# Latent attention of a two-block network: the mask as rows of the score product, and values one unit later

## The reference, cut to what matters

```python
def chunk_ids(L):
    p = jnp.arange(L)
    return jnp.where(p < N_META, 0, 1 + (p - N_META) // CHUNK)      # N_META 16, CHUNK 64
...
    def one_block(args):
        qblk, qc = args
        s = jnp.einsum('bqhd,bkhd->bhqk', qblk, k).astype(jnp.float32) * scale
        mask = cid[None, :] <= qc[:, None]
        p = jax.nn.softmax(jnp.where(mask, s, -jnp.inf), axis=-1).astype(v.dtype)
        return jnp.einsum('bhqk,bkhd->bqhd', p, v)
```

## Time and profile before

| | us |
|---|---|
| median of 3 runs | 2048.93 (2047.54 to 2051.88) |
| the profiled execution's own time | 2042.87 |
| its span, from first to last instruction | 2040.9 |
| PE busy | 1943.8 (95%), 11408 instructions |
| PE's weight loader busy | 1692.7 (83%) |
| DVE busy | 1049.4 (51%) |
| ACT busy | 753.8 (37%) |
| mean granted clock of TensorE | 0.973 |

### The profile page before, as it was taken

One profiled execution on the slowest core, in us unless ns is written; L12 is line 12 of the kernel. 1 busy time (PEld: TensorE's weight loads), 2 busy tenths in 40 slices (PEclk: granted clock), 3 DMA queues, 4 the chain that ended last, 5 costly groups with the idle time before them and its releaser, 6 DMA issues.

```text
span 2040.9 us, 28553 instructions
## 1 busy us (share of the span) xinstructions
PE 1943.8 (95%) x11408; PEld 1692.7 (83%) x11408; DVE 1049.4 (51%) x1480; ACT 753.8 (37%) x1232; POOL 33.0 (2%) x31
## 2 busy tenths in 40 slices
PE   8999998999999997999999999999787999999997
PEld 8887788999999996888888777777686898888886
DVE  5644374664444458544444666676426253323335
ACT  5354342432232434423223425553445352212222
POOL 0100000100000000000000000000000000000000
PEclk9999999999999998999999999999778999999998
DMA  5211101233222332232223232222001223223221
GB/s 180 65 61 42 55 1 52 83 94 93 92 84 92 93 94 93 83 104 93 92 93 94 79 106 73 73 73 83 1 1 63 93 73 103 94 84 102 94 84 61
DMA packets 46607, 161.87 MB, mean 79 GB/s; under 512 B 4832, under 2 KB 7136, under 8 KB 46368
## 3 DMA queue, kind: packets, MB, share of 16 engines
q1 hardware_dynamic: 46208, 158.60, 24.5%
q10 hardware_dynamic: 288, 1.70, 0.2%
HBM read 156.09 MB, written 4.19 MB: 79 GB/s over the span
## 4 chain that ended last, share of the span: by engine, by line
PE 88%; DVE 6%; ACT 3%; DVEq 1%; issue 1%; DMA 0%; ACTq 0%; SPq 0%
PE ps L446 76%; PE ps L944 2%; PE ps L860 1%; DVE wlo L2126 1%; PE ps L964 1%; PE ps L833 1%; DVE W L2519 1%; PE ps L575 1%; PE ps L831 1%; PE ps L1107 1%; DVE AM L2305 1%; PE ps L1070 0%; PE ps L1104 0%; ACT RR L1960 0%; PE ps L1097 0%
## 5 line engine op out<-in xcount | busy, mean ns | idle before, releaser
L446 PE MATMUL ps<-UH,whi 128*128 128x264 f32 (+2 forms) x1920 | 655.1, 341 | 10.7 <-DVE wlo L2126 9.2
L446 PE MATMUL ps<-UL,whi 128*128 128x264 f32 (+2 forms) x1920 | 646.8, 337 | 0.0
L446 PE MATMUL ps<-UH,wlo 128*128 128x264 f32 (+3 forms) x1632 | 530.8, 325 | 0.0
L1351 ACT ACTIVATE whi<-raw 128x1024 fp32r<-128x1024 f32 x284 | 297.8, 1053 | 444.6 <-PE ps L446 424.8
L446 PEld LDWEIGHTS ps<-UH,whi 128*128 128x128 f32 x1920 | 365.0, 190 | 53.2 <-issue 12.6
L446 PEld LDWEIGHTS ps<-UL,whi 128*128 128x128 f32 x1920 | 364.7, 190 | 40.2 <-issue 2.4
L446 PEld LDWEIGHTS ps<-UH,wlo 128*128 128x128 f32 (+1 forms) x1632 | 309.6, 190 | 25.2
L2126 DVE TENSOR_TENSOR wlo<-raw,whi 128x1024 fp32r<-128x1024 f32 x248 | 308.1, 1245 | 39.7 <-ACT whi L1351 39.5
L446 PE MATMUL ps<-HH,whi 128*128 128x264 f32 (+1 forms) x768 | 246.4, 321 | 0.0
L446 PE MATMUL ps<-HL,whi 128*128 128x264 f32 (+1 forms) x768 | 246.3, 321 | 0.0
L446 PE MATMUL ps<-HH,wlo 128*128 128x264 f32 (+1 forms) x768 | 245.7, 320 | 0.0
(11 more groups left out here) (437 smaller groups left out, 2356.3 us busy)
## 6 DMA issues: line engine op xcount, KB each, us to landing
raw<-W SPq DMA_DIRECT2D x284, 512.0 KB, 3.5
H<-xT SPq DMA_DIRECT2D x4, 528.0 KB, 6.5
spill<-H SPq DMA_DIRECT2D x1, 2048.0 KB, 8.9
H<-spill SPq DMA_DIRECT2D x1, 2048.0 KB, 8.6
MEM<-memT ACTq DMA_DIRECT2D x1, 1024.0 KB, 4.7
out<-H SPq DMA_DIRECT2D x2, 512.0 KB, 2.9
out<-H SPq DMA_DIRECT2D x4, 256.0 KB, 3.1
masks<-masks SPq DMA_DIRECT2D x1, 768.0 KB, 9.9
```

The source lines that it names most:

```text
L446: mm = pe.matmul(dst, a, b, start=start and n == 0, stop=stop_ and n == 2)
L1351: act.activation(whi[s % NB][:, :, :], raw[s % NB][:, :, :], ACT.Copy).then_inc(w_hi, 1)
```

## The change

- The queries' rotary rows `QR` and the keys' rotated rows `KRS` become rows 0 to 63 of two tiles of 68 rows, `QRX` and `KRX`. Rows 64 to 67 stand for the four groups of 128 frames. In `QRX` row 64 + g is 1 for the first 64 tokens of group g, in `KRX` it is -1e30 for the last 64 tokens of group g, and both are 0 elsewhere. The product of the two adds -1e30 just where the mask wants it.
- The 20 mask products (16 units, in four of them two) are gone, and `early` with them.
- The four rows come with the rotary table from HBM by two DMAs that ACT issues, one for each tile, each to 4 partitions by 4 heads by 528 tokens. The first score waits for them.
- On PE a unit's place now holds `values(x - 1)`, `score(x + 1)`, `turned(x)`, and `values(19)` comes after the last. On ACT `output(x - 1)` stands ahead of `copies(x)`, and `output(19)` at the end.

```diff
-        early = masks[0:1, LEVELS + 3:LEVELS + 5, :].rearrange("p a t -> p (a t)")[:, 64:64 + P]
...
+        QR, KRS = QRX[0:ROPE, :, :], KRX[0:ROPE, :, :]
...
                 if x:
                     pe.wait_ge(M["exp"], x)
+                else:
+                    pe.wait_ge(rope_in, 48)
...
-                    mm = pe.matmul(flat[0:n, 2048 + a:2048 + b], QR[:, h, q0:q0 + n], KRS[:, h, a:b], start=False,
+                    mm = pe.matmul(flat[0:n, 2048 + a:2048 + b], QRX[:, h, q0:q0 + n], KRX[:, h, a:b], start=False,
                                    stop=True, skip_group_check=True)
-
-                    c = max(a, nk - 64)
-                    if j and c < b:
-                        mm = pe.matmul(flat[0:n, 2048 + c:2048 + b], early, ones[0:1, 0:b - c], start=False, stop=True,
-                                       skip_group_check=True)
...
             def unit(x):
-                turned(x)
+                if x:
+                    values(x - 1)
                 if x + 1 < HEADS * NCH:
                     score(x + 1)
-                values(x)
+                turned(x)
...
                 unit(2 * y + 1)
+            values(HEADS * NCH - 1)
...
             head_rstd(0)
             head_rstd(1)
+            for x, to in enumerate((QRX, KRX)):
+                act.dma_start(to[ROPE:ROPE + 4, :, :], rope_d[ROPE:ROPE + 4, x:x + 1, :].to_broadcast([4, HEADS, L])
+                              ).then_inc(rope_in, 16)
             weights_hi(FT["z3"])
...
             for x in range(HEADS * NCH):
+                if x:
+                    output(x - 1)
                 copies(x)
                 if x + 1 < HEADS * NCH:
                     exps(x + 1)
-                output(x)
...
+            output(HEADS * NCH - 1)
...
+    t, block = np.arange(L)[None, :], META + P * np.arange(4)[:, None]
+    early = np.where((t >= block) & (t < block + 64), 1.0, 0.0)
+    late = np.where((t >= block + 64) & (t < block + P), BIG, 0.0)
+    return np.ascontiguousarray(np.stack([np.concatenate([c, c, early]), np.concatenate([s, s, late])], 1).astype(np.float32))
```

More of the change, by code:

```diff
@@ L183, in build @@
         turn = masks[0:ROPE, LEVELS + 3, 0:ROPE]
-        early = masks[0:1, LEVELS + 3:LEVELS + 5, :].rearrange("p a t -> p (a t)")[:, 64:64 + P]
         future = masks[:, LEVELS + 4, :]
-        ZH, KN, QR, KRS, VT, KR, TAB, SR0, SR1, KSQ, SN, stat = region(
-            S0, ("ZH", [P, 16, L], F32), ("KN", [P, HEADS, L], F32), ("QR", [ROPE, HEADS, L], F32),
-            ("KRS", [ROPE, HEADS, L], F32), ("VT", [P, 5, 512], F32), ("KR", [ROPE, L], F32),
+        ZH, KN, QRX, KRX, VT, KR, TAB, SR0, SR1, KSQ, SN, stat = region(
+            S0, ("ZH", [P, 16, L], F32), ("KN", [P, HEADS, L], F32), ("QRX", [ROPE + 4, HEADS, L], F32),
+            ("KRX", [ROPE + 4, HEADS, L], F32), ("VT", [P, 5, 512], F32), ("KR", [ROPE, L], F32),
             ("TAB", [ROPE, 2, L], F32), ("SR0", [ROPE, L], F32), ("SR1", [ROPE, L], F32), ("KSQ", [ROPE, L], F32),
             ("SN", [ROPE, L], F32), ("stat", [P, 16], F32))
+        QR, KRS = QRX[0:ROPE, :, :], KRX[0:ROPE, :, :]
         hw = S0 + 16 * L * 4
@@ L350, in _ @@
                     sp.dma_start(masks[:, :, :], masks_d[:, 0:LEVELS + 5, :]).then_inc(consts_in, 16)
-            sp.dma_start(TAB[:, :, :], rope_d).then_inc(rope_in, 16)
+            sp.dma_start(TAB[:, :, :], rope_d[0:ROPE, :, :]).then_inc(rope_in, 16)
             sp.dma_start(ABW[:, :, :], gates_d).then_inc(N["ab_in"], 16)
@@ L2995, in constants @@
     turn = np.where(t == s - half, -1.0, 0.0) * (s < ROPE) + np.where(t == s + half, 1.0, 0.0) * (t < ROPE)
-    early = np.where((s == 0) & (t >= 64), BIG, 0.0)
-    masks += [s == t, s <= t, s >= 0, turn + early, np.where(s > t, BIG, 0.0)]
+    masks += [s == t, s <= t, s >= 0, turn, np.where(s > t, BIG, 0.0)]
     for l in range(1, LEVELS + 1):
@@ L3010, in rope_table @@
     c, s = np.cos(ang), np.sin(ang)
-    return np.ascontiguousarray(np.stack([np.concatenate([c, c]), np.concatenate([s, s])], 1).astype(np.float32))
+    t, block = np.arange(L)[None, :], META + P * np.arange(4)[:, None]
+    early = np.where((t >= block) & (t < block + 64), 1.0, 0.0)
+    late = np.where((t >= block + 64) & (t < block + P), BIG, 0.0)
+    return np.ascontiguousarray(np.stack([np.concatenate([c, c, early]), np.concatenate([s, s, late])], 1).astype(np.float32))
 def pack(i):
```

## The result

| | before | after |
|---|---|---|
| median of the timed runs | 2048.23 us (4 runs, 2047.35 to 2051.88) | 2031.66 us (4 runs, 2030.52 to 2035.68) |
| ratio | | 0.9919, 95% interval 0.9901 to 0.9938 |
| profiled execution | 2042.87 us, span 2040.9, clock 0.973 | 2035.68 us, span 2033.4, clock 0.972 |
| first score to the first product of the HGRN scan | 124.80 us | 114.88 us |

The profile shows most of the steps that it named, and two that it did not: shorter groups of transposes, and a fall of the clock just behind the stage.

A forecast was written before the change was run, and what follows sets the result against it. TensorE (PE) was taken as the bound, ending the chain for 88% of the span. PE's work -7.2, waits +0.7 and clock -1.1 gave -7.6 us, applied to the median 2048.93: 2041.3 us, range 2037.0 to 2047.0.

The forecast's parts named there:

- mask products and steps in the score groups: Attention score groups: dropping 20 mask products and using 68 rope rows saves 2.69 us a head, 10.8 us in four.
- 16-row values product: First values product of a unit now follows a 128-row z product, a 0.2 us step in 18 groups: +3.6 us.
- units 9 and 14: Last units of heads 1 and 2: values' waits of 0.55 us go, transposes wait 0.3 more; 0.2 gained each, -0.4.
- unit 19: Last unit: with no score in between, its transposes wait for ACT's output copy, +0.6 us.
- unit 6: Output copy 5 stands behind ACT's scaling and DVE's maximum comes later, so PE waits: +0.5 us.
- unit 4, apart from the clock and the terms above: End of head 0: transposes wait for ACT's output copy behind Silu, but the chain starts sooner; counted as even.
- clock: Attention stage: two paid falls go (-3.0), a likely one at unit 4 (+0.8); half of -2.2 taken, -1.1 us.
- The 0.20 that was to come back: 144-column score group: the step out of the 16-row transposes falls on the z tile behind, returning 0.20 us.
- The first rival: Rope product's load is not pulled ahead, so only the mask products go: -2.4 us, 2046.5 us; chance 0.12.
- The second: Two more clock falls than now are paid, with transposes between short products and z tile: 2045.4 us; chance 0.13.
- The third: ACT's output copy stands behind its side work and delays PE: +11.4 us, 2060.3 us; chance 0.05.
- Waits in sum: PE's waits in the attention stage: heads 1 and 2 -0.4, last unit +0.6, unit 6 +0.5, together +0.7 us.

The follow-up runs named there:

- after_w8: The changed kernel with an already met wait for the rope tables written 9 times instead of once before the first scores; 2037.68 us, 0.9960 of before.
- rows_only: The changed kernel with its mask rows but the order of values and scores from before; 2033.92 us, 0.9946 of before.

## Why the prediction was wrong in size, point by point

The result's own medians lie 16.6 us apart. All runs of the two kernels together give 2044.97 (72 runs) to 2032.31 us (nine), -12.7 us, and by span times clock 1986.7 to 1977.1, -9.6. The lower clock took 56.9 us of a run before and 54.2 after, by the means, another 2.7.

| step | predicted | measured |
|---|---|---|
| mask products and steps in the score groups | -10.8 | -11.2, by differences of starts (-11.0 without the 16-key group) |
| 16-row values product | +3.6 | +3.8, longer values groups and entries |
| transposes ahead of a z tile | not counted | -1.6 |
| units 9 and 14 | -0.4 | -0.8 (0.55 gone, 0.17 new, each) |
| unit 19 | +0.6 | +0.4 |
| unit 6 | +0.5 | 0: no wait at that unit |
| unit 4, apart from the clock and the terms above | 0 | -0.1 (its head takes 32.12 less 2.7 against 31.82, and 2.3 of that are the products) |
| new transfers | 0 | 0 |
| sum without the clock | -6.5 | -9.5 by the rows, -9.6 by the runs |
| clock | -1.1 | -2.7 by the means of all runs, against a scatter of some 10 us of single runs; +2.4 between the two profiled executions |
| sum | -7.6 | -12.2 (-12.7 between the medians) |

The stage's own ends agree: 124.80 less the 3.1 us of its falls, and 114.88 less 2.7, lie 9.5 us apart.

**Right** were the terms that carry the argument: the size of each score group, the step of 0.2 us, that 68 rows behave like 128, and the places of the waits. The load runs 0.42 us ahead of its product, not some 0.1. The 0.20 that was to come back on the z tile behind the 16-row transposes is 0.02 (0.23 against 0.21). The first rival (the rotary product stays a bare one) falls with the load at 139.37. The second (the clock keeps falling) is only half refuted. There is one fall in the stage and not three, and the mean of all runs went the way of the forecast. But both kept executions of the changed kernel pay a second fall behind the stage, which the prediction did not look for when it let nothing downstream move. They have 0.972 as their clock, and six of the nine have 0.973 to 0.975, so not every run need pay it; after_w8, which differs in eight idle waits, has none there. The rival's cause, though, is not what is seen. The short values, transposes and 0.17 us of wait at unit 9 had no fall behind them. By the rule of the Trainium skill's page TensorE: Matmul & The Clock Gate, Part 4 (PE-mode transpose), that transposes do not keep the clock up, as the prediction read it, it would have fallen there. The trace does not bear that reading out for a group of five transposes. The third (ACT's queue on the path) falls with the table of waits: the transposes wait in four units, not in most.

**The steps that failed are three.** First, the sum lacks a term. The prediction costed what each moved group pays on the way in, and not what the group behind it gets. It took the transposes at the length that they had ahead of a score, and they are 1.6 us shorter ahead of a z tile. Second, "Waits in sum: -0.4 + 0.6 + 0.5 = +0.7" was -0.5: unit 6 was a guess between three durations close to one another, and it came out on the free side, while units 9 and 14 gained twice what was taken. These two are 2.8 us of the miss. Third, "I apply the sum to the median" put the forecast on 2048.93 us, the median of three runs, although the profiled execution lay 6.1 us below it. 72 runs have 2044.97, so this base was 4.0 us high, and only 1.5 of uncertainty had been allowed for it. With the 1.6 by which the clock took less than forecast, these make 8.4 of the 9.6 us between forecast and result. That share of the clock is luck in part: in the two profiled executions it went the other way. The rest is inside the scatter of four runs.

That all of the 3.6 us belong to the move was a reason only partly right, with the right number (3.8). The 16-row product pays wherever 68 rows or more stand ahead of it, and without the mask products they do in both orders: in rows_only 0.09 in each of four score groups and 0.17 in the values of a head, 2.1 us in four heads.

## What to carry to other kernels

Count PE's products by what stands next to them, not one by one: here a change from 128 or 68 rows to 64 or 16, or back, costs up to 0.2 us, more than a short product itself, and rows that avoid it (68 for 64, zeros up to 128 for 16) are nearly free. When a group is moved, cost both of its ends and both neighbours. A few runs of a kernel whose clock wanders give a base that is some us off, the span times the granted clock is a finer measure of an edit than the time, and a repeated piece of the trace with no fall in it is finer still. Look for falls also behind the stage that was edited. And where PE's program has loops, look at its instruction packets before an edit is judged: eight idle waits cost more here than the waits that they were to replace.

## What was not expected of the hardware

- **A limit between 64 and 68 rows.** In the same kernel and place the rotary product of 68 rows starts 0.86 us behind a 512-column product with its load 0.42 us ahead, and of 64 rows 0.96 us behind it with no load ahead; over 20 score groups that is 6.6 us by the runs and 5.4 by heads without a fall.
- **A stall of instructions.** Eight more instructions on PE, 440 us ahead of the place, bring nine more packets of 16 KB, all in the loop's second turn, a stall of about 4.2 us where the loop turns, and a clock of 0.57 behind it: 5.3 us in all.
- **The clock by itself.** The share that it takes of a run of the same kernel goes from 46.8 to 65.7 us (72 runs of before), and so two runs of one kernel can differ by more than this change is worth.
